# A weight tile's place in the queue: 16-column projections moved into z's and r's groups, and these cut in thirds

## What is computed

```python
proj = n @ w_in                                   # 1024 x 7712
z, xBC, dt_raw, q, k, v, r, a1, g_ssd, g_gla = jnp.split(proj, idx, axis=-1)
# z 1024, xBC 1536, dt_raw 16, q 512, k 512, v 1024, r 1024, a1 16, g_ssd 1024, g_gla 1024
xBC = silu(causal_dwconv(xBC, conv_w, conv_b))
dt  = softplus(dt_raw + dt_bias)                  # 16 steps a token
y   = (y_diag + y_off + D_skip * x_heads) * silu(z)      # then a norm over each half
log_alpha = log_sigmoid(a1 @ w_a2 + b_a) / 16     # 16 gate columns -> 512
o   = rmsnorm(gla(q, k, v, log_alpha)) * silu(r)
```

## Time and profile before

| | |
|---|---|
| median of 3 runs | 968.85 us (968.66 to 969.35) |
| the profiled execution: its time / its span | 968.41 / 966.6 us |
| PE busy | 958.8 us (99%) |
| DVE busy | 625.5 us (65%) |
| ACT busy | 517.0 us (53%) |
| weights and inputs read | 168.28 MB |

### The profile page before, as it was taken

How to read it: one execution, slowest core, us unless ns; L and a number is a source line. 1 busy time by engine, 2 the same in 40 slices (tenths; PEclk the granted TensorE clock), 3 DMA queues, 4 the chain that set the end, 5 groups by cost and what they waited for, 6 DMA issues and landing times.

```text
span 966.6 us, 15946 instructions
## 1 busy us (share of the span) xinstructions
PE 958.8 (99%) x6548; PEld 869.1 (90%) x6548; DVE 625.5 (65%) x811; ACT 517.0 (53%) x785; POOL 58.1 (6%) x110
## 2 busy tenths in 40 slices
PE   9999999999999999999999999999999999999997
PEld 7877889989988898999988999998998899999996
DVE  5778685777555555778857787776554466555544
ACT  5576554555445444556865665545455445444443
POOL 2000001001000000304000002100000010000001
PEclk9999999999999999999999999999999999999999
DMA  9974536556656566466564465555645347565661
GB/s 303 310 240 127 146 88 176 160 168 203 210 176 190 181 192 194 119 196 195 148 184 142 121 185 186 165 185 172 197 153 170 113 153 218 178 198 175 195 192 45
DMA packets 135528, 170.37 MB, mean 176 GB/s; under 512 B 7856, under 2 KB 99296, under 8 KB 135456
## 3 DMA queue, kind: packets, MB, share of 16 engines
q1 hardware_dynamic: 133488, 165.20, 55.6%
q10 hardware_dynamic: 1424, 2.84, 0.8%
q0 software_dynamic: 544, 1.31, 0.5%
HBM read 168.28 MB, written 1.05 MB: 175 GB/s over the span
## 4 chain that ended last, share of the span: by engine, by line
PE 98%; DVE 1%; issue 0%; ACT 0%; POOLq 0%; DVEq 0%; POOL 0%; ACTq 0%
PE ps L367 15%; PE ps L368 15%; PE ps L369 15%; PE ps L398 8%; PE ps L399 8%; PE ps L400 8%; PE ps L350 5%; PE ps L724 5%; PE ps L725 5%; PE ps L723 5%; PE ps L448 3%; PE ps L479 1%; PE ps L481 1%; PE ps L480 1%; PE ps L613 1%; PE ps L645 1%
## 5 line engine op out<-in xcount | busy, mean ns | idle before, releaser
L1524 DVE TENSOR_TENSOR parts<-raws,parts 128x1024 fp32r<-128x1024 f32 (+2 forms) x309 | 367.7, 1207 | 231.3 <-ACT parts L1020 230.6
L1020 ACT ACTIVATE parts<-raws 128x1024 fp32r<-128x1024 f32 (+2 forms) x309 | 316.2, 1040 | 238.5 <-PE ps L369 137.5
L367 PE MATMUL ps<-room_r,parts 128*128 128x256 f32 x1248 | 352.2, 282 | 0.0
L368 PE MATMUL ps<-room_r,parts 128*128 128x256 f32 x1248 | 348.5, 279 | 0.0
L369 PE MATMUL ps<-room_r,parts 128*128 128x256 f32 x1248 | 348.3, 279 | 0.0
L367 PEld LDWEIGHTS ps<-room_r,parts 128*128 128x128 f32 x1248 | 234.6, 188 | 5.6 <-issue 3.9
L368 PEld LDWEIGHTS ps<-room_r,parts 128*128 128x128 f32 x1248 | 234.7, 188 | 1.3
L369 PEld LDWEIGHTS ps<-room_r,parts 128*128 128x128 f32 x1248 | 234.6, 188 | 0.0
L398 PE MATMUL ps<-parts,room_r 128*128 128x512 f32 (+1 forms) x336 | 134.8, 401 | 0.5 <-DVE parts L1524 0.5
L400 PE MATMUL ps<-parts,room_r 128*128 128x512 f32 (+1 forms) x336 | 131.1, 390 | 0.0
L399 PE MATMUL ps<-parts,room_r 128*128 128x512 f32 (+1 forms) x336 | 131.0, 390 | 0.0
(11 more groups left out here) (225 smaller groups left out, 875.7 us busy)
## 6 DMA issues: line engine op xcount, KB each, us to landing
raws<-in_w_in SPq DMA_DIRECT2D x99, 512.0 KB, 4.4
raws<-in_w_ffn_in SPq DMA_DIRECT2D x44, 512.0 KB, 4.2
raws<-in_w_up SPq DMA_DIRECT2D x32, 512.0 KB, 4.4
raws<-in_w_down SPq DMA_DIRECT2D x32, 512.0 KB, 4.3
raws<-in_w_ffn_out SPq DMA_DIRECT2D x22, 512.0 KB, 4.2
raws<-in_w_xkv SPq DMA_DIRECT2D x16, 512.0 KB, 4.3
raws<-in_w_out SPq DMA_DIRECT2D x8, 512.0 KB, 4.4
raws<-in_w_up_ssd SPq DMA_DIRECT2D x8, 512.0 KB, 4.6
```

What stands on the lines that cost most here:

```text
L367: e.matmul(ps, wh, hT[0][:, k, :], start=k == 0, stop=False)
L368: e.matmul(ps, wh, hT[1][:, k, :], start=False, stop=False)
L1020: e.activation(t.h, t.raw, ACT.Copy).then_inc(s["hi"], 1)
L1524: e.tensor_tensor(t.l, t.raw, t.h.bitcast(F32), ALU.subtract).then_inc(s["lo"], 1)
```

## The change

It does five things. The 16 columns of dt and the 16 of the gate are no longer projected by `narrow`: the weight tiles of z's first group carry dt's columns behind their own, those of r's first group the gate's (`also`, two loads a tile). z and r are made in three groups of 336, 352 and 336 columns (`spans=THIRDS`) instead of two of 512, so their tiles have 704 words (2 x 352) or 672 (2 x 336) and there are 12 of each instead of 8. ScalarE copies dt out of z's first group and the gate's columns out of r's (`thirds_out`), the latter twice, into columns 0 and 32 of `twice`; one transpose of 48 rows gives `a1T` in two strips, and the gate's products alternate between the strips. The two exponentials of the dt chain stand behind z's first group. The scaling of x stands behind the silu of block 2, ahead of the last convolution block. The steps between the named work are dealt out anew (2, 2, 3, 3, 3 around the convolution blocks, before 1, 2, 2, 2, 2).

```diff
+        THIRDS = [(0, 336), (336, 352), (688, 336)]
...
-            fill = chain(tm("z", w2, 0, 1024, xT, x_ready(MIX2)), fm("gq", w2, 2576, 512, xT, x_ready(MIX2)),
+            fill = chain(tm("z", w2, 0, 1024, xT, x_ready(MIX2), spans=THIRDS, also=2560), fm("gq", w2, 2576, 512, xT, x_ready(MIX2)),
...
-                         tm("r", w2, 4624, 1024, xT, x_ready(MIX2)), fm("sig2", w2, 5664, 2048, xT, x_ready(MIX2)),
+                         tm("r", w2, 4624, 1024, xT, x_ready(MIX2), spans=THIRDS, also=5648), fm("sig2", w2, 5664, 2048, xT, x_ready(MIX2)),
...
-            step()
+            step(2)
             conv()
             spread_rstd(4, MIX2)
-            narrow("a1dt", [(w2, 5648), (w2, 2560)], xT, x_ready(MIX2))
-            step(2)
-            b = bank()
-            out_of("a1dt")
-            for t in range(2):
-                last = e.transpose(psum[:, b, 16 * t:16 * t + 16], a1T[32:48, t * P:t * P + P], ident[32:48, 32:48])
-            ends(last, "dt", b)
-            conv()
             step(2)
             conv()
-            step(2)
+            step(3)
             conv()
-            step(2)
+            step(3)
+            conv()
+            step(3)
...
-                step()
+                step(2 if i in (5, 6) else 1)
                 if i == 7:
                     y_out(0, 1)
+                    need(s["a1"], 2)
+                    turn("a1T", [twice[:, half_, 0:48] for half_ in range(2)])
...
-            step(3)
+            step(5)
             y_out(1, 1)
             step()
-            need(s["wa2"], 16)
-            for i in range(2):
-                b = bank()
-                for c in range(2):
-                    h = 2 * i + c
-                    last = group(psum[:, b, 256 * c:256 * c + 256], [(wa2[:, h * P:h * P + P], a1T[0:16, :])])
-                ends(last, ("la", i), b)
+            need(s["wa2"], 32)
+            out_of("a1T")
+            own = [bank() for _ in range(2)]
+            for c in range(2):
+                for i in range(2):
+                    h, strip = 2 * i + c, slice(32 * i, 32 * i + 16)
+                    last = group(psum[:, own[i], 256 * c:256 * c + 256], [(wa2[strip, h * P:h * P + P], a1T[strip, :])])
+                    if c:
+                        ends(last, ("la", i), own[i])
...
+            def thirds_out(dst, name, f, more, more_to):
+
+                for blk, (c0, n) in enumerate(THIRDS):
+                    halves_ = [where[name, blk, t] for t in range(2)]
+                    yield halves_[1].at
+                    e.wait_ge(s["pe"], halves_[1].at)
+                    if blk == 0:
+                        for t, g in enumerate(halves_):
+                            to = more_to(t)
+                            e.activation(to, bc(psum[:, g.bank, n:n + 16], 1, list(to.shape)), ACT.Copy,
+                                         scale=scaled(MIX2, t)).then_inc(s[more], 1)
+                    for t, g in enumerate(halves_):
+                        e.activation(dst[:, t, c0:c0 + n], psum[:, g.bank, 0:n], f, scale=scaled(MIX2, t)).then_inc(taken[g.bank], 1)
...
-            until(where["a1dt"].at + 1)
-            for t in range(2):
-                e.wait_ge(s["zrstd"], t + 1)
-                e.activation(x[:, t, :], z[:, t, :], ACT.Copy, scale=rstd[sq_of[MIX2]][t]).then_inc(s["y"], 1)
             conv_in(2)
+            until(where["z", 0, 1].at + 1)
             e.wait_ge(s["rows"], 80)
             e.activation(Aexp, row("ssd_A_log_2"), ACT.Exp).then_inc(s["Aexp"], 1)
-            full("dt")
...
             silu(2)
+            for t in range(2):
+                e.wait_ge(s["zrstd"], t + 1)
+                e.activation(x[:, t, :], z[:, t, :], ACT.Copy, scale=rstd[sq_of[MIX2]][t]).then_inc(s["y"], 1)
             conv_in(5)
```

More of the change, by code:

```diff
@@ L47 @@
     "ret_sq", "ret_rstd", "ret", "oT_hi", "retT_hi", "gates", "mix", "mix_hi", "mixT", "up", "up_hi", "upT",
-    "pad", "conv_in", "conv", "silu", "gated", "Aexp", "dt", "soft_e", "soft_exp", "soft_sq", "soft", "a", "a_twice", "sel", "cs_hi", "decays", "X", "Xd", "E",
+    "pad", "conv_in", "conv", "silu", "gated", "Aexp", "dt", "soft_e", "soft_exp", "soft_sq", "soft", "a", "a_twice", "a1", "sel", "cs_hi", "decays", "X", "Xd", "E",
     "y_sq", "y_sum", "y_rstd", "y_out", "yT_gain", "yT_hi", "yT", "la", "la_min", "la_ln", "bcum", "bexp", "qt", "kt",
@@ L331, in ends, with weight @@
                 fifo.append(b)
[L333 removed]
+            def weight(src, k, n, paired=False, also=None):
                 i = len(tiles)
@@ L376, in fm, with tm, tile_at @@
                     yield
-            def tm(name, w, c0, cn, hT, ready, ahead=False, first=0, depths=None):
+            def tm(name, w, c0, cn, hT, ready, ahead=False, first=0, depths=None, spans=None,
+                   also=None):
                 K = w.shape[0] // P
                 depths = depths or [2] * (K // 2)
-                for b0 in range(512 * first, cn, 512):
-                    nb = min(512, cn - b0)
+                spans = spans or [(b0, min(512, cn - b0)) for b0 in range(512 * first, cn, 512)]
+                for blk, (b0, n) in enumerate(spans, first):
+                    more = blk == 0 and also is not None
+                    nb = n + 16 if more else n
                     own = [bank(), bank()]
-                    tile_at = lambda k0, deep: weight(w[k0 * P:(k0 + deep) * P, c0 + b0:c0 + b0 + nb], deep, nb)
+                    def tile_at(k0, deep):
+                        rows_ = slice(k0 * P, (k0 + deep) * P)
+                        return weight(w[rows_, c0 + b0:c0 + b0 + n], deep, nb, also=w[rows_, also:also + 16] if more else None)
                     asked = None
@@ L401, in tm @@
                             if not next_deep:
-                                ends(last, (name, b0 // 512, t), own[t])
+                                ends(last, (name, blk, t), own[t])
                         w_.release = done(last) if next_deep else count
@@ L1892, in vector @@
             conv_in(1)
-            full("a1dt")
-            emptied(tt(a1T[0:48, :], bank_of("a1dt")[0:48, 0:256], rows_rstd[0:48, :], ALU.mult), "a1dt")
             conv(0)
             conv_in(2)
-            until(where["a1dt"].at + 1)
+            until(where["spread", MIX2].at + 2)
             conv(1)
-            full("dt")
-            emptied(tt(dt3, bank_of("dt")[:, 0:32].rearrange("p (t h) -> p t h", t=2),
-                       bc(row("ssd_dt_bias_2"), 1, [P, 2, 16]), ALU.add), "dt")
-            out_of("dt")
+            until(where["z", 0, 1].at + 1)
+            e.wait_ge(s["dt"], 2)
+            step(tt(dt3, dt3, bc(row("ssd_dt_bias_2"), 1, [P, 2, 16]), ALU.add))
+            settle()
             stt(e_, dt_, -1.0, dt_, ALU.mult, ALU.min).then_inc(s["soft_e"], 1)
@@ L2023, in vector @@
                     y_T(*((0, 0), (1, 0), (0, 1))[i // 2 - 1])
+                if i == 6:
+                    full("a1T")
+                    emptied(e.tensor_copy(a1T[0:48, :], bank_of("a1T")[0:48, 0:256]), "a1T")
             y_T(1, 1)
```

24 lines of the change are left out of this document (14 added, 10 removed).

## The result

The changed kernel takes **979.37 us** (median of 4 runs, 979.05 to 979.48), the kernel before took 969.1 us on the same chip (4 runs, 968.66 to 969.68). The ratio is 1.0107, with a 95% interval of 1.0095 to 1.0119: slower by 10.3 us, or 1.1%. The forecast was 976.5 us, range 969.5 to 981: 8.1 us more than the kernel before. The span of the profiled execution grew by 10.9 us, from 966.6 to 977.5.

A forecast was written before the change was run, and what follows sets the result against it. PE was taken as the bound: its matmuls plus its waits for weight tiles. Own work of -3.2 us and waits of 1.7 + 4.3 + 2.3 + 3.0 = 11.3 gave +8.1 on 968.41: 976.5 us, range 969.5 to 981.

The forecast's parts named there:

- PE's own work: Matmul and transpose time on PE without waits: removed, added and overlapped work sum to -3.2 us.
- no fixed part that matters: PE's matmuls of 256 or more columns: cost goes with columns alone, 0.456 ns each, so thirds add nothing.
- The first wait: PE at convolution block 4's first weight tile, split at 433.93 on VectorE: 1.7 us late.
- The second: PE at convolution block 4's second weight tile, behind conv(3) in VectorE's queue: 4.3 us late.
- The third wait: PE at convolution block 5's second tile, behind conv(4) on VectorE, silu and x's scalings on ScalarE: 2.3 us late.
- rival 4: PE's clock falls to 1.2 GHz in the 4.3 us wait: 977.5 to 980 us, chance 0.08.
- The gate: Behind the gate's products, five tiles instead of three precede yT's product on VectorE; PE's tile comes 3.0 us late.
- the case given 0.58: Whole kernel as forecast, 976.5 us within 2.5 us; chance 0.58.
- the rule: PE's clock: an idle array falls back to half clock, adding some 1 to 3 us; left out of the sum.
- Rival 1: The saving goes through, every weight tile reaching PE in time: 965.2 us, chance 0.09.
- Rival 2: Only VectorE's own work counts, ScalarE never waited for: waits of 2.7 to 5, 968 to 970.5 us, chance 0.10.
- rival 3: Waits at the convolution come as worked out, the one at the gate does not: 973.5 us, chance 0.15.

The follow-up runs named there:

- experiment 1: Changed kernel plus 34 useless fp32 identity products on PE ahead of convolution block 4's second weight tile; 979.41 us.
- experiment 10: Changed kernel with experiments 3, 6 and 9, and block 4's first tile let in ahead of the exponentials, dt's two instructions and conv(2); 967.85 us.
- experiment 11: experiment 10 with dt's two VectorE instructions moved ahead of the split that VectorE waits for at 427.5; 967.71 us.
- experiment 3: Changed kernel with the second weight tile of blocks 4 and 5 rounded and split ahead of the previous block's conv_in and conv; 972.92 us.
- experiment 6: Changed kernel with the tile VectorE waits for at 424.2 rounded on ScalarE ahead of conv_in(2); 978.02 us.
- experiment 4: Changed kernel with the two scalings of x moved on ScalarE back ahead of conv_in(3); 978.59 us.
- experiment 2: Changed kernel plus 19 useless fp32 identity products on PE ahead of convolution block 4's second weight tile; 976.79 us.
- experiment 5: Changed kernel with four steps of r instead of five ahead of y's last transpose, and two instead of one behind; 978.0 us.
- experiment 7: Changed kernel with four steps of r, y's last transposes, the gate's products at once, then ten steps; 980.98 us.
- experiment 9: experiment 5 with the gate's additions on VectorE waiting only for their products, so a split comes behind them; 975.12 us.
- experiment 8: Changed kernel with the edits of experiments 3, 4, 6 and 7 together; 974.01 us.

## Why the prediction was right, and where its sum was off

The growth can be read off at marks on PE that both kernels pass. These are the marks behind the change's first stage and at the products behind the gate, before and after; those at the gate's products themselves before are in the earlier trace rows.

```profile
458.38 0.38 PE L448 MATMUL ps<-ident,room 128*128 128x128 f32 x2
...
566.91 0.34 PE L350 MATMUL ps<-room 128*64 128x64 f32 x2
```

```profile
465.23 0.27 PE L442 MATMUL ps<-ident,room 128*128 128x128 f32 x1
...
549.98 1.13 PE L356 MATMUL ps<-room,wa 16*128 16x256 f32 x8
551.04 0.39 PE L373 MATMUL ps<-room_r,parts 128*128 128x256 f32 x1
...
577.04 0.34 PE L356 MATMUL ps<-room 128*64 128x64 f32 x2
```

| stretch | grew by | forecast | made of |
|---|---|---|---|
| z and the convolution, 407.3 to 465.2 | +6.85 | +5.4 | waits 6.6, half clock 2.6, slow matmuls behind waits 0.2, own work -2.6 |
| to the gate's products, 550.0 | +0.73 | +0.6 | 16 columns of r, two transposes |
| the eight passes of the gate | -0.86 | -0.9 | 1.92 became 1.06 |
| to the products behind, 577.0 | +3.40 | +3.0 | waits 1.84, 0.54, 0.70, slow matmuls behind them 0.25 |
| to the end | +0.8 | 0 | 0.38 is a wait at 588.8 |

The first matmul behind a wait holds PE for 0.19 to 0.22 us, where the others of its kind take 0.117; the forecast had no such term. Half clock is 13.84 less 11.20 us of experiment 1.

**PE's own work, forecast -3.2 us: measured -2.7.** The eight passes overlap in pairs, as L613 had it. The columns were dearer: two z tiles of 352 columns took 3.90 us, 407.32 to 411.23, where 0.456 ns a column gives 3.85. Over 16 wide and 8 narrow tiles, thirds and added columns cost 1.2 us instead of 0.7. A matmul of 352 columns came every 0.163 us and not every 0.160, and one of 336 every 0.154 and not every 0.153. This is the term that "no fixed part that matters" had put at nothing. In experiments 10 and 11, where only one wait is left and the clock stays up, the first stretch gives the same -2.6.

**The first wait, 1.7: measured 1.86. The second, 4.3: measured 4.15.** conv(0) started at 421.11 (forecast 421.06), the waited-for tile at 426.08 (its rounding was forecast to end at 426.05), conv(3) at 435.92 (435.8). Experiments 3 and 6 show the mechanism: take conv(3) out from ahead of the tile, and the second wait is gone; give VectorE its tile 1.9 us sooner, and only 0.67 arrive, because ScalarE's queue bounds.

**The third wait, 2.3: measured 0.61, and 1.40 at full clock.** The mechanism held (in experiment 4 the wait goes with the scaling of x), the size did not. Part of it was eaten by the half clock, which made PE late too; this the forecast had foreseen for its rival 4. The rest, 0.9 us, is in part PE's own work up to there, some 0.4 longer than forecast, and in part a tile that was split some 0.5 sooner.

**The gate, 3.0: measured 3.1, and 0.4 behind it.** The chain's additions started at 554.91. The steps named were the right ones, the reload of the fifth tile's buffer among them. Here ScalarE waits for it:

```profile
550.50 1.06 ACT L1012 ACTIVATE parts<-raws 128x1024 fp32r<-128x1024 f32 x1 [2.19 <-DMA raws<-in_w_in]
```

This rounding starts 0.52 us behind the gate's products (549.98), and the first wait is 1.84. In experiment 2 it starts 0.28 ahead of them (548.73) and the wait is 1.03, in experiment 1 0.40 ahead and 0.91, in experiment 4 0.81 behind and 2.13: each time the wait is this distance plus 1.31 to 1.32. So the landing of that load sets the first wait at the gate, and 0.8 of the 2.6 us that experiment 2 won came through it. But the sum left out that VectorE then works without a gap from 564 to 576, so that one late start shows as four waits. Experiments 5, 7 and 9 show the cause: with the additions at 550.6 and splits let in behind them nothing is left; with the same additions and no splits it gets worse.

**The clock, rival 4, given 0.08 and 977.5 to 980: it came true on top of the forecast.** This is the step that failed: the time lies in the stated range, but 2.9 us above 976.5, so outside the 974 to 979 of the case given 0.58 and inside rival 4's. The sum of the others alone would have given about 976.8, which is what experiment 2 took. That this is so near to 976.5 is in part luck: in that run the third wait was 0.9 us shorter than forecast and the waits at the gate 0.7 (2.3 us together), while own work was 0.5 us more, the slow matmuls behind waits some 0.4, and the stretch past 577 some 0.8. "By the row the sum stays at +8.1; by the rule it is some 1 to 3 us more" was the choice made, and the row chosen was one from behind the last matmul, which says nothing of a wait of 4 us inside the program; the trace of before held no such wait. The rule decided: the Trainium skill (TensorE: Matmul & The Clock Gate, The HAM clock gate) says that an idle array falls back to half its clock, and this case's runs agree for this wait, with 0.53 granted in 440 to 446 behind it and 1.00 where PE was kept at work; what the shorter waits did stands in the last section. The 2.6 us that keeping PE at work won, 1.8 of them in the convolution, are within the 1 to 3 that were worked out and not taken.

Rival 1, the saving going through, needed another order: it is what experiments 10 and 11 approach. They come 0.85 and 1.16 us under the kernel before; 2.7 us of own work saved less the wait of 1.56 or 1.22 us would give 1.1 and 1.5, 0.3 more. Rival 2 (VectorE's own work alone) is refuted by the trace, in which VectorE waits 1.90 and 1.22 us for ScalarE, rival 3 (no wait at the gate) by the three waits there.

What stays open: why the same wait of 4.15 us was followed by 6.8 us at half clock in some kernels and 3.4 us in others; why the load at the gate lands earlier against PE in some kernels; and the 0.4 us that the rest of the kernel behind 588.8 is longer. The experiments show that order makes the loss and takes it away. They don't show which of the change's five parts made the old order unfit: no run has the thirds without the added columns, or a deeper stock of tiles. That the smaller tiles did it is argued from the order of the queues.

## What to carry to other kernels

Tiles made smaller also shorten the time that a stock of a fixed number of them covers: by the working above, 5 tiles of which three are short no longer reached over a convolution on VectorE in the old order, and every queue that fills the stock had to be ordered anew. Read the due time of each tile against the two queues that make it; a tile that stands behind a long block of unrelated work is moved ahead of it when the block would wait anyway. A chain whose steps are hooked to tile counts moves against the tiles when its start is moved, so move the start and look at what it leaves uncovered. And when a forecast holds a wait of some microseconds of TensorE, its clock belongs into the sum.

## What was not expected of the hardware

- Useless work made the kernel faster: 4.2 us of identity products in a wait of 4.15 us won 2.6 us, of which 1.8 because the clock stayed at its 2.4 GHz level (1.00 granted) and 0.8 because a load at the gate came earlier against PE.
- The clock did not answer to each wait alike. A wait of 3.24 us (experiment 8) left it at full, one of 3.26 us at the same place (experiment 7) was followed by a stretch at 1.2 GHz, and so was one of 2.13 us (experiment 4), while those of 1.84 us (the changed kernel, at the gate) and 1.87 us (experiment 3) were not.
- An fp32 product of 128 columns took 0.22 us in two passes; that is nearly the time of a 512-column product in fp32r (0.23 us, 12 in the 2.79 us of the earlier trace rows).
